# The parameters and the first operand of a transformer kernel are loaded from another engine's queue

## The reference, cut to what matters

```
def rmsnorm(x, g):
    xf = x.astype(jnp.float32)
    y = xf * lax.rsqrt(jnp.mean(xf * xf, axis=-1, keepdims=True) + EPS)
    return (y * g.astype(jnp.float32)).astype(x.dtype)
...
        a = rmsnorm(h, attn_norm[i])
        proj = a @ w_in[i]
```

## Time and profile before

| | us |
|---|---|
| median of three runs | 2269.01 |
| lowest and highest of the three | 2268.60, 2269.14 |
| the profiled execution, whole | 2269.67 |
| span of its instructions | 2268.0 |
| PE busy in the span | 2245.2 |
| ACT busy, DVE busy | 1157.0, 1915.4 |

### The profile page before, as it was taken

The page is one execution under the profiler, slowest core; times in us unless marked ns, Lnnn a source line. Parts: engine busy times, 40 slices in busy tenths (PEclk is TensorE's granted clock), DMA queues, the critical chain, the costliest instruction groups (busy, mean ns, idle before and its releaser), DMA issues.

```text
span 2268.0 us, 36924 instructions
## 1 busy us (share of the span) xinstructions
PE 2245.2 (99%) x13898; PEld 2024.6 (89%) x13898; DVE 1915.4 (84%) x3130; ACT 1157.0 (51%) x1708; POOL 109.2 (5%) x208
## 2 busy tenths in 40 slices
PE   8999999999999999999999999999999999999998
PEld 7989898888888888888899899989988888888887
DVE  7988989899999999999989878998777677677776
ACT  6554665555445354454457668556633434434335
POOL 0000000000111111111010000000000000000000
PEclk9999999999999999999999999999999999999999
DMA  8556664568888888888885554556555555555553
GB/s 316 183 180 239 237 211 150 183 241 300 288 299 302 298 300 292 308 298 301 297 287 192 200 202 149 187 203 223 187 192 194 189 186 187 189 195 191 186 186 112
DMA packets 86414, 513.67 MB, mean 226 GB/s; under 512 B 9685, under 2 KB 10245, under 8 KB 37360
## 3 DMA queue, kind: packets, MB, share of 16 engines
q1 hardware_dynamic: 57456, 406.88, 50.0%
q0 software_dynamic: 28656, 104.33, 13.8%
q10 hardware_dynamic: 144, 0.26, 0.0%
HBM read 509.30 MB, written 2.13 MB: 225 GB/s over the span
## 4 chain that ended last, share of the span: by engine, by line
PE 93%; DVE 4%; ACT 2%; issue 0%; DMA 0%; SPq 0%; DVEq 0%; ACTq 0%
PE ps L558 39%; PE ps L567 21%; PE ps L620 10%; PE ps L625 5%; PE ps L617 3%; PE ps L616 3%; PE ps L618 3%; DVE wl L1603 1%; PE ps L689 1%; PE ps L646 1%; PE ps L647 1%; PE ps L645 1%; PE ps L699 1%; PE ps L770 1%; PE ps L718 1%
## 5 line engine op out<-in xcount | busy, mean ns | idle before, releaser
L1044 ACT ACTIVATE wh<-raw 128x1024 fp32r<-128x1024 f32 x766 | 792.8, 1053 | 655.3 <-PE ps L567 471.9
L1603 DVE TENSOR_TENSOR wl<-raw,wh 128x1024 fp32r<-128x1024 f32 x762 | 928.7, 1220 | 187.0 <-ACT wh L1044 175.7
L558 PE MATMUL ps<-xs,wh 128*128 128x512 f32 x1688 | 411.1, 391 | 0.0
L558 PEld LDWEIGHTS ps<-xs,wh 128*128 128x128 f32 x1688 | 307.5, 189 | 57.7
L1711 DVE CUSTOM_DVE_ANT_0 modraw<-modraw,cb 128x1024 f32<-128x1024 f32 x192 | 233.6, 1219 | 10.9 <-DMA modraw<-in_wmod 10.7
L620 PE MATMUL ps<-xs,wh 128*128 128x512 f32 x936 | 237.2, 395 | 0.0
L567 PEld LDWEIGHTS ps<-xs,wl 128*128 128x128 f32 x1688 | 222.1, 191 | 11.6
L567 PE MATMUL ps<-xs,wl 128*128 128x256 f32 x1688 | 225.7, 282 | 0.0
L1698 DVE SCALAR_TENSOR_TENSOR x<-ps,mod,x 128x256 f32<-128x256 f32 x320 | 154.2, 482 | 76.5 <-PE ps L567 70.4
L620 PEld LDWEIGHTS ps<-xs,wh 128*128 128x128 f32 x936 | 168.3, 189 | 31.5 <-issue 0.6
L558 PE MATMUL ps<-xc,wh 128*128 128x512 f32 x696 | 172.0, 389 | 0.5 <-ACT wh L1044 0.5
(11 more groups left out here) (355 smaller groups left out, 3285.3 us busy)
## 6 DMA issues: line engine op xcount, KB each, us to landing
raw<-in_w SPq DMA_DIRECT2D x381, 1024.0 KB, 5.0
modraw<-in_wmod POOLq DMA_DIRECT2D x192, 512.0 KB, 4.8
x<-in_x SPq DMA_DIRECT2D x4, 512.0 KB, 8.6
raw<-in_w SPq DMA_DIRECT2D x4, 512.0 KB, 9.1
tbias<-rel_rows POOLq DMA_DIRECT2D x4, 512.0 KB, 5.8
cb<-c_silu POOLq DMA_DIRECT2D x1, 1024.0 KB, 5.1
out_dram<-ytok SPq DMA_DIRECT2D x2, 512.0 KB, 3.4
hmask<-in_hmask SPq DMA_DIRECT2D x1, 512.0 KB, 16.9
```

Of the source, the lines that this page charges most:

```text
L558: nc.tensor.matmul(PS[(b + bi) % 4][:, :], hi[:, t * P:(t + 1) * P], src[k].rearrange("p a t -> p (a t)"), start=first and n == 0, stop=la ...
L1044: nc.scalar.activation(wh[:, h % HS, :], raw[:, u % RAW, (h % 2) * 1024:(h % 2 + 1) * 1024], ACT.Copy).then_inc(s_round, 1)
L1603: nc.vector.tensor_tensor(wl[:, h % HS, :], raw[:, (h // 2) % RAW, (h % 2) * 1024:(h % 2 + 1) * 1024], wh[:, h % HS, :].bitcast(F32), ALU. ...
```

## The change

The load of the parameters (`par`) and the four loads of x's quarters are taken out of SP's list and put into ACT's. `par` and quarter 0 stand ahead of ACT's table load; quarters 1 to 3 follow the small activation, ahead of the wait for the parameters. SP's list now begins with the four halves of the first two weight units. Semaphores, tiles and sizes stay.

```
         @block.sync
         def _(sp):
-            def load_x(g):
-                sp.dma_start(x[:, 4 * g:4 * g + 4, :], a["x"][:, 4 * g:4 * g + 4, :]).then_inc(s_x[g], 16)
-
-            sp.dma_start(par[:, :], a["par"]).then_inc(s_par, 16)
-            load_x(0)
             sp.dma_start(raw[:, 0, 0:1024], a["w"][0, :, 0:1024]).then_inc(s_w0, 16)
-            load_x(1)
             sp.dma_start(raw[:, 0, 1024:2048], a["w"][0, :, 1024:2048]).then_inc(s_raw[0], 16)
             sp.dma_start(raw[:, 1, 0:1024], a["w"][1, :, 0:1024]).then_inc(s_w2, 16)
             sp.dma_start(raw[:, 1, 1024:2048], a["w"][1, :, 1024:2048]).then_inc(s_raw[1], 16)
-            load_x(2)
-            load_x(3)
...
+            def load_x(g):
+                act.dma_start(x[:, 4 * g:4 * g + 4, :], a["x"][:, 4 * g:4 * g + 4, :]).then_inc(s_x[g], 16)
+
+            act.dma_start(par[:, :], a["par"]).then_inc(s_par, 16)
+            load_x(0)
             act.wait_ge(s_ones, 1)
             nc.scalar.activation(small[:, 36:37], ones[:, 0:1], ACT.Copy)
+            for g in range(1, 4):
+                load_x(g)
             act.wait_ge(s_par, 16)
             entry_x(0)
             rnd(0)
```

## The result

The changed kernel takes **2272.01 us** (median of 22 runs, 2270.57 to 2277.27) against 2269.12 for the kernel before (22 runs beside them). The ratio is 1.0013, 95% interval 1.0008 to 1.0019, which is 3.0 us slower, between 1.8 and 4.3 (the two medians are 2.9 apart). The profiled execution took 2271.4 us, 1.7 more than the profiled one of before; its span is 2269.7 against 2268.0.

A forecast was written before the change was run, and what follows sets the result against it. PE, busy 99% of the span, was taken as the bound, so its first matmul's delay moves the end. Quarter 0 at 10.15 plus 2.84 gave 12.99 instead of 10.08, +2.9: median 2269.01 + 2.9 = 2271.9 us, range 2268.3 to 2273.5.

The forecast's parts named there:

- landing plus 2.84 us: At the start: PE's first matmul comes 2.84 us after quarter 0 lands, if the weights are already there.
- turns by packet: In the DMA engines: two full queues alternate packet by packet, a packet being a tile row, so each advances one load.
- w0b with quarter 0: At the start: the first weight unit's second half lands together with quarter 0, at 1736 KB, quarter 0 4.4 us later.
- The size of the term: Arrival order at the start: quarter 0 at 10.15 us, PE at 12.99 instead of 10.08, +2.9 us.
- rival A: Loads from 3.4 to 8.9 us: a second queue lifts the rate, +0.2 us; 0.28 shared with D and all between.
- D: At the start: first half of weights and quarter 0 both land near 8.9, PE +1.7 us; 0.28 shared with rival A.
- Quarter 3: x's last quarter lands with the next full weight unit at 19.7 us, ACT's entry moves 1.9 us, covered by PE's delay.
- Issues on ACT: Head of ACT's list: the moved DMA issues leave ACT free at 4.6 us, at worst 8.4, and cost nothing.
- The first sixteen matmuls run slowly: PE's first matmuls: they move with the start and cost the same, put at nothing, with 0.3 us either way.
- POOL's stream: POOL waits for the second weight unit's second half, begins 1.3 us later; PE is later by more, so no effect.
- B: At the start: queues don't share, only issue time changes; PE 0.9 us early, time 2268.3; chance 0.12.
- C: At the start: the weight queue gets two rows for one of ACT's, PE at 15.6, +5.5 us, 2274.5; chance 0.06.

The follow-up runs named there:

- hold_weights: Changed kernel, with SP issuing the first half of weights, then waiting for x's quarter 0 before all later weight loads; 2271.35 us, ratio 1.0006.
- rows_8k: Changed kernel, with the first two weight units loaded in one DMA each, rows of 8 KB instead of two times 4 KB; 2273.75 us, ratio 1.0016.
- w0_first_on_act: Changed kernel, with ACT rounding the first half of weights ahead of x's quarter 0; 2271.30 us, ratio 1.0008.
- one_queue_weights_first: Kernel before, all loads still on SP but in the order in which the changed kernel's loads land; 2272.01 us, ratio 1.0010.
- only_x123_on_act: Changed kernel, with parameters and quarter 0 back at the head of SP's queue, only quarters 1 to 3 on ACT; 2270.59 us, ratio 1.0003.
- needed_first_on_both: Changed kernel, with quarter 0 first on SP, parameters first on ACT, first half of weights split by columns over both queues; 2269.91 us, ratio 1.0000.
- again: Changed kernel, unchanged, timed and profiled a second time; 2271.62 us, ratio 1.0011.
- after_third: Changed kernel, unchanged, timed and profiled a third time; 2272.00 us, ratio 1.0012.

## Why the prediction was right

**The bound: right.** One wait of PE, ahead of its first matmul, was to grow and nothing behind it. A rest of 2231.1 or 2231.2 in eleven profiles shows it.

**The rule "landing plus 2.84 us": right.** Landing to PE start: 9.2 to 12.05; 8.1 to 10.99 (hold_weights); 10.7 to 13.56 (rows_8k); 10.0 to 12.82 (one queue). That ACT's order makes it was shown by w0_first_on_act.

**The turns by packet: right.** "w0b with quarter 0" landed as 8.9 with 9.2; the earlier trace rows had been a good row to rest it on, though it is of POOL's queue and not ACT's, and rows_8k tells it from turns by bytes and from turns by load. That quarter 0 gives turns to both halves of weights, where it had stood ahead of them, is the loss; hold_weights puts 1.1 us of its 3.4 on what follows the first half.

**The size of the term: too large.** The prediction put quarter 0 at 10.15 us because it took the delivery of the kernel before, 1736 KB at 10.2 us. It came at 9.2. That is rival A, "two queues fill the slow stretch", in part: 357 GB/s, not the 420 it would need, and +2.1 at PE's start in the means of three, not +0.2 and not +2.9. By PE's start the outcome lies in the part that the prediction gave to A and D (+0 to +2.3, 0.28) and not in the forecast's own (+2.3 to +3.6). Its signs say the same: quarter 0 was to land at 9.5 to 10.5 and ACT to idle for some 7 us, and it was 9.2 and 6.0. one_queue_weights_first shows that most of the gain came with the second queue (290 to 357 GB/s) and little with the order (269 to 290). The forecast of the time, 2271.9, lies 0.1 from the measured 2272.01, nearer than its working earns: the start gave 2.1 instead of 2.9, the end of PE's slow rate on the average 0.2, and the rest is the spread of medians (the two later sets gave +2.2). That it came so near is luck.

**Quarter 3: direction right, size off.** It was to land at 19.7 with a pause of ACT; it landed at 18.2 with a pause of 0.26 us, covered by PE's late start as said.

**Issues on ACT: covered, otherwise than told.** I had the three further issues behind the small activation, up to 8.4 us at worst. They ran from 1.87 to 3.74, and began beside the table load (1.80 to 3.08). The cover (idle until 9.3) was never touched.

**"The first sixteen matmuls run slowly ... nothing, with 0.3 us either way": too narrow.** The slow rate ended 3.7 (only_x123_on_act) to 6.1 us (needed_first_on_both) behind PE's start. Counted from PE's start, the body mark moved by up to 0.7 us between executions of one program (26.2 to 26.9 in the kernel before, 26.5 to 27.2 in the changed one).

**POOL's stream: no effect, otherwise than told.** It was to begin 1.3 us later; it began at 14.30, before at 14.29.

**Rivals.** B fell with quarter 0 at 9.2. The Trainium skill, "DMA: Bandwidth & Descriptors", section "Issuing engines are not separate DMA queues", has two halves: the transfers interleave on the same engines, which these runs show (8.9 with 9.2; 7.5 for 5.8 in only_x123_on_act), and several issuers save only issue time, which the runs don't bear out for the first 9 us (357 against 290 GB/s for the same order of arrival) and do behind them (423 against 420). C fell too: the queues took equal turns. D's numbers are those of A's middle; its reason, both near 8.9, was wrong, since the first half of weights was in at 6.4.

## What to carry to other kernels

Moving loads to a second queue does not put them aside: here it let them take every second turn, so ask of each load what will stand beside it in the other queue and how long that queue's rows are. Before advancing a load, check which of the inputs the consumer's instruction order takes up first; here the load that was advanced waited 4.5 us for the one it delayed. And where PE is full behind its start, the start is paid one for one: a mark at the first steady matmul splits a difference of 2 us into start and rest better than timed runs do.

## What the runs showed of the hardware that I had not expected

- Between 3.4 and 8.9 us of this program one queue moved 269 to 290 GB/s, two full queues with 4 KB rows and 128 partitions 357 to 360, with the first half of weights in rows of 2 KB 313, with 8 KB rows on one of them 393; behind 8.9 us most versions moved 411 to 425. Two queues with the first half of weights and quarter 1 in loads of 64 partitions moved 269.
- Two full queues took turns of one row on each DMA engine, whatever the length of the row: 211 and 213 packets in 5.5 us with 1.60 and 0.55 MB (rows_8k), and 16 of each in 0.6 us on 16 engines.
- PE's first matmuls take 0.43 us for 512 columns and the later ones 0.23, while the granted clock reads 1.00, the upper level of 2.4 GHz, in every stretch looked at; the profile's clock column doesn't show the slow rate, and what ends it these runs don't say. The end of the slow rate moved between 16.9 and 18.0 us in three executions of one program that began PE at 12.02 to 12.05 us.
- ACT's sequencer issued DMAs while its table load of 1.28 us (1.80 to 3.08) ran: in `again` and `after_third` two, from 1.87 us on, with the third begun at 3.30 and 3.23; in only_x123_on_act the first at 1.18 us, beside a table load from 0.88 on.
